# Head sums of squares in the second projection: one float32 matmul replaced by two rounded matmuls over a split square

## What is computed

```python
def odd_layer(x, g_pre, g_post, w_in, q_norm, k_norm, w_out):
    h = rms_norm(x, g_pre)
    proj = jnp.einsum('btd,de->bte', h, w_in)
    q, k, v, gate = jnp.split(proj, SPLIT_C, axis=-1)
    q = rms_norm(q.reshape(B, T, C_HEADS, C_HEAD_DIM), q_norm)     # 16 heads of 64
    k = rms_norm(k.reshape(B, T, C_KV_HEADS, C_HEAD_DIM), k_norm)  #  4 heads of 64
    q = jnp.concatenate([rope(q[..., :half], rows), rope(q[..., half:], cols)], axis=-1)
    k = jnp.concatenate([rope(k[..., :half], rows), rope(k[..., half:], cols)], axis=-1)
```

## Time and profile before

| | |
|---|---|
| median of 3 runs | 2231.22 us (2229.95 to 2232.13) |
| the profiled execution | 2227.72 us, of which its span 2225.9 us |
| PE busy | 2063.4 us, 93% of the span |
| DVE busy | 1290.8 us, 58% |
| ACT busy | 1121.6 us, 50% |
| POOL busy | 1099.6 us, 49% |
| mean granted TensorE clock | 0.971 |

### The profile page before, as it was taken

The page is one execution under the profiler, slowest core; times in us unless marked ns, Lnnn a source line. Parts: engine busy times, 40 slices in busy tenths (PEclk is TensorE's granted clock), DMA queues, the critical chain, the costliest instruction groups (busy, mean ns, idle before and its releaser), DMA issues. The chain is left out here.

```text
span 2225.9 us, 25137 instructions
## 1 busy us (share of the span) xinstructions
PE 2063.4 (93%) x9332; PEld 1635.3 (73%) x9332; DVE 1290.8 (58%) x1896; ACT 1121.6 (50%) x1427; POOL 1099.6 (49%) x549
## 2 busy tenths in 40 slices
PE   6999998899999999999975899998999999998996
PEld 5878876778888877777754677897777777775784
DVE  7243144325777676684546477723477777888444
ACT  6042234335555666674315444333477777777431
POOL 5433445434555555564005677734466666666300
PEclk9999999999999999999987999999999999999998
DMA  4133477416555554454345133253233233323434
GB/s 170 50 121 130 143 286 280 129 58 139 118 113 107 110 126 112 93 165 159 96 131 213 57 113 114 104 155 93 67 69 78 67 78 72 78 79 108 164 100 142
DMA packets 170794, 266.58 MB, mean 120 GB/s; under 512 B 75744, under 2 KB 84576, under 8 KB 170672
## 3 DMA queue, kind: packets, MB, share of 16 engines
q1 hardware_dynamic: 170672, 264.97, 41.3%
HBM read 167.01 MB, written 97.91 MB: 119 GB/s over the span
## 5 line engine op out<-in xcount | busy, mean ns | idle before, releaser
L2119 POOL TENSOR_TENSOR c_PL<-c_PF,c_PH 128x1024 fp32r<-128x1024 f32 x128 | 309.6, 2419 | 159.3 <-ACT c_PH L1882 89.7
L2119 POOL TENSOR_TENSOR ab_PL<-ab_PF,ab_PH 128x1024 fp32r<-128x1024 f32 (+3 forms) x128 | 276.1, 2159 | 187.6 <-ACT ab_PH L1882 125.8
L1879 ACT ACTIVATE ab_PF<-ab_SA 128x1024 f32<-128x1024 f32 (+3 forms) x160 | 143.6, 898 | 172.9 <-PE ab_SA L1678 98.1
L1879 ACT ACTIVATE c_PF<-c_SA 128x1024 f32<-128x1024 f32 x160 | 163.9, 1024 | 103.8 <-PE c_SA L1717 103.4
L1954 DVE TENSOR_REDUCE c_MH<-c_SM 128x1 f32<-128x512 f32 x256 | 172.5, 685 | 70.2 <-PE c_SM L1643 69.6
L1882 ACT ACTIVATE c_PH<-c_PF 128x1024 fp32r<-128x1024 f32 x128 | 135.7, 1060 | 4.1
L1717 PE MATMUL c_SA<-c_Q,c_KA 128*128 128x512 f32 x320 | 129.4, 404 | 7.5 <-ACT c_PF L1879 7.5
L365 POOL TENSOR_TENSOR e_wl<-e_raw,e_wh 128x1024 fp32r<-128x1024 f32 (+1 forms) x31 | 72.8, 2349 | 128.3 <-ACT e_wh L525 128.3
L1643 PE MATMUL c_SM<-c_KA,c_Q 128*128 128x512 f32 x320 | 126.0, 399 | 5.8 <-DVE c_MH L1954 3.9
L1717 PE MATMUL c_SA<-c_Q,c_KB 72*128 72x512 f32 x320 | 128.6, 402 | 0.0
L1882 ACT ACTIVATE ab_PH<-ab_PF 128x1024 fp32r<-128x1024 f32 (+3 forms) x128 | 119.6, 935 | 4.0
(11 more groups left out here) (457 smaller groups left out, 6123.2 us busy)
## 6 DMA issues: line engine op xcount, KB each, us to landing
c_Q<-qC_hi SPq DMA_DIRECT2D x32, 384.0 KB, 4.9
e_raw<-in_w_tiles SPq DMA_DIRECT2D x20, 512.0 KB, 3.9
n_raw<-in_w_tiles SPq DMA_DIRECT2D x18, 512.0 KB, 3.7
e_XF<-in_xT SPq DMA_DIRECT2D x12, 512.0 KB, 9.4
silu_gate<-e_ta SPq DMA_DIRECT2D x24, 256.0 KB, 2.0
ab_Q<-qA_hi SPq DMA_DIRECT2D x16, 384.0 KB, 5.3
ab_G<-silu_gate SPq DMA_DIRECT2D x24, 256.0 KB, 3.6
ab_res<-in_xT SPq DMA_DIRECT2D x24, 256.0 KB, 2.9
```

The source lines that it names most:

```text
L1879: nc.scalar.activation(used(PF[p], h, s), used(SA, h, s), ACT.Exp).then_inc(e_done, 1)
L2119: nc.gpsimd.tensor_tensor(used(PL[p], h, s), used(PF[p], h, s), used(PH[p], h, s).bitcast(F32), ALU.subtract).then_inc(p_lo[0], 1)
```

## The change

`tsq` stays a float32 square. ACT adds a rounded copy of it (`thi`), DVE the difference (`tlo`, written over `tsq`), and PE multiplies `headsel`, now in rounded form, with both, into the same PSUM bank. `headsel` is loaded in float32 and rounded once by ACT, after the sigmoid of unit 4.

```diff
-            pe.wait_ge(q_sq, i + 1)
+            pe.wait_ge(q_hi, i + 1)
             wait_count(pe, q_log, i - 1)
-            nc.tensor.matmul(sums[i % 2], sel[:], tsq[i % 2][:], start=True, stop=True).then_inc(q_sum, 1)
+            nc.tensor.matmul(sums[i % 2], sel[:], thi[i % 2][:], start=True, stop=False)
+            pe.wait_ge(q_lo, i + 1)
+            nc.tensor.matmul(sums[i % 2], sel[:], tlo[i % 2][:], start=False, stop=True).then_inc(q_sum, 1)
...
             nc.scalar.activation(tsq[i % 2][:], ta[i % 3][:], ACT.Square).then_inc(q_sq, 1)
+            act.wait_ge(q_sq, i + 1)
+            nc.scalar.activation(thi[i % 2][:], tsq[i % 2][:], ACT.Copy).then_inc(q_hi, 1)
...
+            if n == 4:
+                act.wait_ge(tab_in, 96)
+                nc.scalar.activation(sel[:], sel_in[:], ACT.Copy).then_inc(sel_set, 1)
...
+        def low_square(n):
+            i = qk.index(n)
+            dve.wait_ge(q_hi, i + 1)
+            nc.vector.tensor_tensor(tlo[i % 2][:], tsq[i % 2][:], thi[i % 2][:].bitcast(F32), ALU.subtract
+                                    ).then_inc(q_lo, 1)
+
...
             if n - 1 in qk and n != v0:
                 finish(n - 1)
+            if n in qk:
+                low_square(n)
             if n - 2 in qk and n < v0:
                 low(n - 2)
```

More of the change, by code:

```diff
@@ L782, in inner @@
     mm_done, acc_read = ar.sem("n_mm_done"), ar.sem("n_acc_read")
-    q_sq, q_sum, q_log, q_rstd = (ar.sem(f"n_q_{n}") for n in ("sq", "sum", "log", "rstd"))
+    q_sq, q_hi, q_lo, q_sum, q_log, q_rstd = (ar.sem(f"n_q_{n}") for n in ("sq", "hi", "lo", "sum", "log", "rstd"))
+    sel_set = ar.sem("n_sel_set")
     r_swap, r_cos, r_sin, r_sum, r_norm = (ar.sem(f"n_r_{n}") for n in ("swap", "cos", "sin", "sum", "norm"))
@@ L808, in inner @@
     tsd = [at(f"tsd{i}", [P, CH], F32, REST + 45056 + 2048 * i) for i in range(2)]
-    sel = at("headsel", [P, P], F32, REST + 49152)
+    sel_in, sel = at("headsel_in", [P, P], F32, REST + 49152), at("headsel", [P, P], F32R, REST + 49664)
+    thi = [at(f"thi{i}", [P, CH], F32R, REST + 50176 + 2048 * i) for i in range(2)]
+    tlo = [at(f"tlo{i}", [P, CH], F32R, REST + 40960 + 2048 * i) for i in range(2)]
     rtok = at("rtok", [P, TT], F32, SMALL)
@@ L872, in sync @@
         sp.dma_start(hg[:], A["g_heads"]).then_inc(tab_in, 16)
-        sp.dma_start(sel[:], A["headsel"]).then_inc(tab_in, 16)
+        sp.dma_start(sel_in[:], A["headsel"]).then_inc(tab_in, 16)
         for i in range(4):
@@ L972, in head_sums @@
             if i == 0:
-                pe.wait_ge(tab_in, 96)
+                pe.wait_ge(sel_set, 1)
             if i < 2:
                 pe.wait_ge(deviation, NC)
-            pe.wait_ge(q_sq, i + 1)
+            pe.wait_ge(q_hi, i + 1)
             wait_count(pe, q_log, i - 1)
-            nc.tensor.matmul(sums[i % 2], sel[:], tsq[i % 2][:], start=True, stop=True).then_inc(q_sum, 1)
+            nc.tensor.matmul(sums[i % 2], sel[:], thi[i % 2][:], start=True, stop=False)
+            pe.wait_ge(q_lo, i + 1)
+            nc.tensor.matmul(sums[i % 2], sel[:], tlo[i % 2][:], start=False, stop=True).then_inc(q_sum, 1)
         def token_scales():
```

## The result

The changed kernel takes 2258.0 us (median of 4 runs, 2252.6 to 2261.3) against 2231.7 (4 runs): ratio 1.0110, 95% interval 1.0098 to 1.0123. It was run again as e0: 2256.6 against 2234.5, ratio 1.0096 (1.0081 to 1.0112). By the two ratios it is slower by 24.5 us (21.9 to 27.5) and by 21.5 us (18.1 to 25.0); forecast were 21.2.

A forecast was written before the change was run, and what follows sets the result against it. PE was taken to bound the q/k stage, the ring only 0.3 us per tile faster. Nine tiles of 21.3 us plus two units of 6.3 give 204.3, +21.2 us, so 2252.4 us (+0.95%); range 2244 to 2268.

The forecast's parts named there:

- PE stops being the bound, its saving is lost: q/k head sums: PE saves 0.40 us per unit, 12.0 over 30, worth nothing beyond 0.3 us per tile.
- the ring: DVE, ACT and POOL waiting on each other in the q/k stage: 18.72 us per three-unit tile, against PE's 19.02.
- ACT's copy, +0.66 us ahead of L1200: One more ACT activation per q/k unit, between square and Ln: L1200's inputs come 3.36 us after the eviction, not 2.70.
- DVE's subtraction: One more two-input DVE operation per q/k unit, after L1200: waits out POOL's product in L1206's place; L1206 then runs free.
- the layout: q/k eviction intervals with both additions: 6.3 us plain, 8.0 ahead of a tile's weights, 7.0 after; 21.3 per tile.
- `headsel`'s rounding costs nothing: A 128-column ACT operation ahead of a weight copy that waited 3.22 us for POOL: no cost.
- The sum: First to last q/k eviction: nine tiles of 21.3 us and two units of 6.3, 204.3 against 183.15, +21.2 us.
- The rival: PE's clock falls in every q/k tile as PE idles: +7 to +22 us on top, 2260 to 2275; chance 0.15.
- The sign that was named for it: Sign of the clock rival: a PE clock below 1.00 between 1257 and 1460 us.
- Nothing after the stage changes: After the last q/k eviction: the rest of the span unchanged to a us or two.
- The Trainium skill's short idles: Rule that short idles between matmul groups make PE's clock swing; followed to the letter, it makes the clock rival the forecast.

The follow-up runs named there:

- e4: Kernel before with ACT writing the square rounded and one rounded head-sum matmul, low part of the squares left out: 2227.0 us against 2233.6, ratio 0.9972.
- e1: Changed kernel with ACT's copy and DVE's subtraction kept, but the one float32 head-sum matmul of the kernel before: 2257.8 us against 2234.5, ratio 1.0099.
- e3: Kernel before plus only a DVE subtraction (square minus a constant tile, result unused), no rounded copy: 2265.7 us against 2234.5, ratio 1.0142.
- e7: Changed kernel with the subtraction's first operand read from PSUM, low part of the squares left out: 2245.9 us against 2233.6, ratio 1.0050.
- e8: As e7, with DVE's low part of q or k also reading PSUM, those low parts left out: 2233.9 us against 2233.6, ratio 0.9998.
- e9: Kernel before, full computation, with only DVE's low part of q or k moved right behind the eviction: 2233.8 us against 2233.3, ratio 1.0003.
- e5: As e4, with DVE's low part of q or k moved right behind the eviction: 2215.6 us against 2233.6, ratio 0.9922.

## Why the prediction was right

**PE stops being the bound, its saving is lost.** Right: the ring's 18.72 us a tile, read off three evictions, came back in e4. e1 shows it from the other side. The 0.46 us for the two matmuls shows where evictions still wait for PE, at the start of the stage: the products alone take 5.44 us (1258.94 to 1264.38), with the two matmuls 5.89, with the float32 one of e1 6.35, with e4's single one 5.67 (1261.97 to 1267.64). So two cost 0.45 and one 0.23, and the saving is 0.46 a unit where 0.40 were forecast.

**ACT's copy, +0.66 us ahead of L1200.** Right: L1210 comes 3.37 us after the eviction (1320.67 - 1317.30), laid out were 3.36; alone, the copy makes tiles of 20.1. Beside the subtraction it adds next to nothing (e3 without its clock falls, 204.8, against 204.5).

**DVE's subtraction.** Right in kind and size: intervals of 6.34, 8.04 and 7.00 against 6.3, 8.0 and 7.0 in the layout, and e7 and e8 show that it is the ports. I had said that the subtraction would take 1.7 us where L1206 was: in plain intervals it is L1210 that waits (1.64), and the subtraction takes 0.68; its median is 1.65.

**`headsel`'s rounding costs nothing.** The wait it stood in shrank to 3.02 us, from 3.22; nothing moved behind it.

**The sum.** 21.2 us were forecast for the stage; it grew by 21.3 in e0, 21.9 in e1 and 23.2 in the first profile. I had counted nine equal tiles. In e0 the first took 22.6 us (DVE scales tables there), the second 20.7 and the last, with half-width weights behind it, 20.5: they cancel.

**The clock.** The rival was right in kind and, for the change, far too large. The sign that was named for it, a clock below 1.00 in the stage, did come. But the clock was to fall in every tile; in the first profile it fell around 1290 (0.84) and once more, and that stage is 1.9 us longer than e0's. In e0 it fell in two tiles (0.92 in each) and no eviction waited for it. In e3 the rival's price came true: 1.45 us for each fall that reached an eviction, where 0.8 to 2.5 had been laid out.

The 5.6 us by which the time is over the forecast are mostly not the stage; in the second comparison, with 22.1 us between the medians, the excess over 21.2 is 0.9. Between kernels the profiled executions differ outside the stage by up to 12.5 us (e8), and by 11.8 between the kernel before and e9, whose q/k stages are equal:

```profile
core 0: 2237.7 us, clock 0.966
```

Its span is 11.8 us more and its mean clock 0.966 against 0.971. Span times what the clock lacks to 1 is the time lost: 2237.7 x 0.034 = 76.1 us against 2225.9 x 0.029 = 64.6, 11.5 more. So here the numbers put the difference down to the clock (the means have three digits, so each product is good to 1 us). For every kernel it does not hold: e7's late start is not the clock's. "Nothing after the stage changes" was right for the work and wrong for the single execution.

The Trainium skill's short idles ("TensorE: Matmul & The Clock Gate", "A second HAM failure mode: psum-queue depth-cycling") did show, but in the change not as the rule would have it: its PE idles in every tile (21.6 us of 181) and keeps a clock of 1.00 in most, as from 1300 to 1321. e1, where PE had more work in the same ring, had 1.00 throughout. e3 comes nearer to the rule, with five tiles at 0.92 to 0.93 and 0.96 over the stage.

## What to carry to other kernels

Read the period of the next-slowest ring, not the busy share of its engines: here DVE was 77% busy and its ring 1.6% faster than PE, so moving work from PE to it could gain 0.1 us a unit and lost 0.7. Where DVE and POOL both work on SBUF, price an added two-input operation by what it may have to stand behind, and look whether one operand can stay in PSUM. When two bounds lie so close, a step against one shows next to nothing until the other is lowered too. And before a longer stage is put down to the ring, look at the clock and at which evictions wait for PE: a quarter of e3's cost was that.

## What the runs showed that was not expected

One addition alone (the subtraction, +28.9 us) costs more than it does together with another (+21.3). Of the 28.9, 7.2 us are falls of PE's clock; the 21.7 that are left by this estimate are what both additions cost together, so the copy, 7.9 us alone, is hidden. In the kernel before, DVE's low part moved up gains nothing; once PE's bound is lowered it gains 10 us (e5 against e4). On the change, ACT's move gains nothing alone, and 14 us together with DVE's. And two executions with equal work in the stage differ by 12 us of span, by these numbers through the clock alone, more than half of the effect that was studied: the length of the stage told in one profile what the whole time told only over many runs.
